# Depthwise convolution of two channel tiles: one matmul per two taps and 64 channels, or four column groups of 32 channels with four taps in the rows

## The chip, the core and the metric

The kernel runs on one core of a Trainium2 chip. The metric is the device time of one execution in microseconds (us). The core's engines run side by side and meet at semaphores: TensorE (PE, with its weight loads shown apart as PEld), VectorE (DVE), ScalarE (ACT), GpSimd (POOL), and SyncE (SP), which here only issues DMAs.

## What is computed

A trunk of two layers over 528 positions (16 meta tokens and 512 frames) of 1024 channels, in float32. The change lies in layer 0's mixer, whose convolution group is, cut to what matters:

```python
z = h @ w_in                                   # 1024 -> 1536
a = a_in[..., :512] * sigmoid(a_in[..., 512:]) # GLU
lhs = pad(a, 30 zeros in front)                # causal
a = conv(lhs, w[31, 512], one filter per channel) + b
a = silu(layer_norm(a, g, b))                  # over the 512 channels
...                                            # pool group p, 4 groups of 128
return concatenate([a, p]) @ w_out
```

So each of the 512 channels is filtered with its own 31 taps. After this mixer come a feed-forward block, a gated linear attention layer, a second feed-forward block and a last norm; they are not touched.

## The kernel before, in words

Channels lie on the 128 partitions, positions in the free dimension; the 512 convolution channels are four tiles `c` = 0 to 3 (`CT`), each 128 channels by 528 positions (`TOK`). Nearly all products are "exact" ones: both operands are split into a high and a low part (`w_hi`, `w_lo`, `u_hi`, `u_lo`), and three matmuls replace one (`exact`, L1863). ACT makes the high parts (`split_hi`, L531), DVE the low ones (`split_lo`, L538), from blocks that SP loads into `raw`, two buffers deep. PSUM has four slots (`NS`); a slot is filled by PE in the order of `plan_slots`, and PE begins slot n only when n-4 has been evacuated. Each engine's order is written out by hand, as one instruction stream.

PE's order in the mixer: for each `c` two projections (`glu`), with the transposes of the small vectors (L1991, L1992) after the first, and a transpose of the input (`flip_x`); then `conv_taps(2)`; the four pool projections `p`; `conv_taps(3)`, into whose middle `mix(0)` and `mix(1)` are put (`MIX_BEFORE`); `mix(2)`, `mix(3)`; then eight `outp` products, with `mean` after the third and `var` after the fifth; then eight `outc` products.

Where the taps run. Tiles 0 and 1 are done on DVE, one instruction for each tap over the tile (`run_taps`, L1356, the instruction at L1372 and for tap 0 at L1363), 62 in all. Of tile 2 DVE does 14 taps and PE 17, and PE does all 31 of tile 3. On PE a tile is taken as two groups `g` of 64 channels. `x_phase` holds the even positions of a group in one half of the partitions and the odd ones in the other half (`split_phases`, four ACT copies a tile, L838); `diag` holds, for each step, a 128 by 128 matrix of four diagonals with the taps (`build_diags`, two ACT instructions a step, L809, with `ident_half` and `cw_phase`); one matmul of 264 columns (L2009) is a step, 18 of them for tile 2 and 32 for tile 3, float32 without a split. ACT adds the bias and sorts even and odd positions back (`evac_conv`, four instructions a tile, L873).

`mean` needs the sum of all four tiles: DVE writes `conv_sum` in two additions (L1421, L1432), and PE waits for them and for tile 2's last tap (L2043 to L2045).

Of the kernel before, what the change touches and what calls it, by code (L numbers as in the profile page):

```python
# [20 lines left out]
P = 128  # L21
# [34 lines left out]
PHASE = P // 2  # L56
SHIFTS = {2: 9, 3: 16}
PE_TAPS = [(c, t) for c in SHIFTS for t in range(2 * SHIFTS[c] - 1)]
PE_STEPS = [(c, g, j) for c in SHIFTS for g in range(2) for j in range(SHIFTS[c])]
DIAGS = 28  # L60

MIX_BEFORE = 16
# [5 lines left out]
CONV_STEP, POOL_STEP, MIX_STEP, OUT_STEP = 11, (0, 3, 3, 0), (0, 0, 1, 0), 2  # L68
# [138 lines left out]
def build_trunk(nc, x, meta_tokens, mix_norm_g, ffn_norm_g, ffn_w1, ffn_w2, cp_w_in, cp_conv_w,  # L207
                cp_conv_b, cp_ln_g, cp_ln_b, cp_pool_w, cp_pool_scale, cp_w_out, gla_w_in,
                gla_gate_w2, gla_gate_b, gla_head_g, gla_w_out, final_norm_g, out):
    with ExitStack() as ctx:  # L210
# [47 lines left out]
        with ExitStack() as part:  # L258
# [13 lines left out]
            with ExitStack() as mixer0:  # L272
                win = sb("win", [P, 2, WMAX + TOK], F32, mixer0)
                rcount = sb("rcount", [P, WMAX], F32, mixer0)
                pw = sb("pw", [P, PG, P], F32, mixer0)
                pw_hi = sb("pw_hi", [P, PG, P], F32R, mixer0)
                pw_lo = sb("pw_lo", [P, PG, P], F32R, mixer0)


                conv_in = sb("conv_in", [P, CT, TAPS - 1 + TOK], F32, mixer0)  # L280
                conv = sb("conv", [P, CT, TOK], F32, mixer0)
                x_phase = sb("x_phase", [P, 2, 2, (TAPS - 1 + TOK) // 2], F32, mixer0)
                cw_phase = sb("cw_phase", [P, 2, 2, (TAPS + 1) // 2, 2], F32, mixer0)
                cb_phase = sb("cb_phase", [P, 2, 2], F32, mixer0)
                ident_half = sb("ident_half", [P, PHASE], F32, mixer0)
                diag = sb("diag", [P, DIAGS, 2, PHASE], F32, mixer0)
                gw2_raw = sb("gw2_raw", [P, DK], F32, mixer0)
# [40 lines left out]
        conv_sum, centred_sq_sum = h_sq[:, 0, :], h_sq[:, 1, :]  # L328
# [46 lines left out]
        x_phase_ready = sem("x_phase_ready")  # L375
        cw_phase_ready = sem("cw_phase_ready")
        phase_consts = sem("phase_consts")
        diag_ready = sem("diag_ready")
        diag_used = sem("diag_used")
# [61 lines left out]

        def diag_free(eng, i):

            c = PE_STEPS[i][0]
            if i + 1 == len(PE_STEPS) or PE_STEPS[i + 1][0] != c:
                filled(eng, SLOT["conv", c])
            else:
                eng.wait_ge(diag_used, i + 1 - (c - 2))
# [158 lines left out]
        def _(sp):  # L607
# [88 lines left out]
        def _(pool):  # L696
# [17 lines left out]
            pool.memset(ident_half[:, :], 0.0).then_inc(phase_consts, 1)  # L714
            for half in range(2):
                pool.wait_ge(phase_consts, 1 + half)
                pool.affine_select(out=ident_half[:, :], in_=ident_half[:, :], compare_op=ALU.not_equal,
                                   fill=1.0, base=-PHASE * half, pattern=[[-1, PHASE]],
                                   channel_multiplier=1).then_inc(phase_consts, 1)
            pool.memset(cw_phase[:, :, :, :, :], 0.0).then_inc(phase_consts, 1)  # L720

        @block.scalar
        def _(act):
# [65 lines left out]
            act.activation(vec[:, 2 * KD:], ps[:, n % NS, 0:NV - 2 * KD], ACT.Copy)  # L789
            act.activation(cw[:, :], ps[:, n % NS, BANK:BANK + TAPS * CT], ACT.Copy)\  # L790
# [9 lines left out]
            built = [0]  # L800

            def build_diags(count):

                for i in range(built[0], min(built[0] + count, len(PE_STEPS))):
                    c, g, j = PE_STEPS[i]
                    if i >= DIAGS:
                        diag_free(act, i - DIAGS)
                    for b in range(2):
                        last = act.activation(diag[:, i % DIAGS, b, :], ident_half[:, :], ACT.Copy,  # L809
                                              scale=cw_phase[:, c - 2, g, j, b:b + 1])  # L810
                    last.then_inc(diag_ready, 1)
                    built[0] = i + 1

            def half(i):
                return slice(PHASE * i, PHASE * (i + 1))

            def set_phases():

                taps = cw[:, :].rearrange("p (t c) -> p c t", c=CT)
                act.wait_ge(phase_consts, 4)  # L820
                for g in range(2):
                    for a in range(2):
                        act.activation(cb_phase[half(a), :, g], vec[half(g), V_CB + 2:V_CB + CT], ACT.Copy)
                        for b in range(2):
                            for c, shifts in SHIFTS.items():
                                first, last = (1 if a < b else 0), (shifts - 1 if a > b else shifts)
                                t = 2 * first + a - b
                                n = last - first
                                ins = act.activation(cw_phase[half(a), c - 2, g, first:last, b],
                                                     taps[half(g), c, t:t + 2 * n - 1:2], ACT.Copy)  # L830
                ins.then_inc(cw_phase_ready, 1)
                act.wait_ge(cw_phase_ready, 1)

            def split_phases(c):

                for g in range(2):
                    for a in range(2):
                        last = act.activation(x_phase[half(a), c - 2, g, :], conv_in[half(g), c, a::2], ACT.Copy)  # L838
                last.then_inc(x_phase_ready, 1)
# [8 lines left out]
            for c in range(CT):  # L848
# [7 lines left out]
                build_diags(6 if c else 0)  # L856
# [4 lines left out]
                if c == 0:  # L861
                    set_phases()
                if c >= 2:
                    evacuated(act, SLOT["glu", 2 * c + 1])
                    split_phases(c)

            def evac_conv(c):
# [3 lines left out]
                for g in range(2):  # L871
                    for b in range(2):
# [5 lines left out]
            build_diags(sum(c == 2 for c, _, _ in PE_STEPS) - built[0])  # L878
            evac_conv(2)
            for g in range(PG):  # L880
# [3 lines left out]
                build_diags(8 if g == 0 else 4)  # L884
                if g % 2:
                    split_hi(2 * B_POOL + g + 3)
                    split_hi(2 * B_POOL + g + 4)
                    for i in (g - 1, g):
                        act.wait_ge(pd_ready, i + 1)
                        act.activation(a_hi[:, i, :], work[i], ACT.Copy).then_inc(pd_hi_ready, 1)  # L890
                        if i == PG - 2:
                            build_diags(6)
# [7 lines left out]
            for g in range(PG):  # L900
                if g == 2:
                    build_diags(len(PE_STEPS))
                mix_hi(g)
            evac_conv(3)
# [1472 lines left out]
```

## Time and profile before

| | us |
|---|---|
| time, median of 3 runs | 1107.4 |
| time, lowest and highest | 1106.69, 1107.47 |
| span of the profiled execution | 1105.6 |
| PE busy | 1091.0 |
| PE weight loads busy | 1019.9 |
| DVE busy | 811.0 |
| ACT busy | 562.8 |
| POOL busy | 4.6 |

The span runs from the first to the last instruction of the one execution that was profiled. Busy time says how long an engine had an instruction in it; matmuls are pipelined, so a busy PE can still hide waste. The time of a stage is therefore read from the chain that ended last and from the timeline, and the work of a stage from groups of instructions.

### The profile page before, as it was taken

To read this page: it belongs to the slowest core of one execution; us is meant where nothing else is said; L and a number is where in the kernel's file an instruction comes from. 1 tells how busy PE (TensorE), PEld (TensorE's weight loads), DVE (VectorE), ACT (ScalarE), POOL (GpSimd) and SP (SyncE) were. 2 spreads that over 40 slices of the span, in tenths; PEclk is the share of its full clock that TensorE was granted. 3 is DMA by queue.
4 is the path that set the end of the run, shared out by engine and by line. 5 is a ranking of instruction groups with operands and counts; after the bars stand their busy time and mean duration, and the time that the engine had idled before them with its cause. 6 is when DMAs were issued, how large, how long until landed. Compare 5 with 4: busy or idle time off the path is not lost.

```text
span 1105.6 us, 18616 instructions
## 1 busy us (share of the span) xinstructions
PE 1091.0 (99%) x7649; PEld 1019.9 (92%) x7649; DVE 811.0 (73%) x1166; ACT 562.8 (51%) x933; POOL 4.6 (0%) x34
## 2 busy tenths in 40 slices
PE   7999999999999999999999999999999999999997
PEld 6999999999999999999999788787898898899897
DVE  6889987786786785789463456756796786786885
ACT  6658455454454454466642234534464454454564
POOL 1000000000000000000000000000000000000000
PEclk9999999999999999999999999999999999999999
DMA  7321122135134124223223211223134134234221
GB/s 213 116 76 49 58 76 88 40 115 152 39 115 129 63 83 146 77 77 114 77 78 95 75 61 39 69 84 110 43 115 147 45 115 123 68 100 130 77 76 78
DMA packets 98929, 100.39 MB, mean 91 GB/s; under 512 B 2834, under 2 KB 95692, under 8 KB 98844
## 3 DMA queue, kind: packets, MB, share of 16 engines
q1 hardware_dynamic: 98780, 99.12, 28.5%
q8 instruction: 61, 1.00, 0.4%
q14 instruction: 24, 0.20, 0.1%
q10 hardware_dynamic: 64, 0.07, 0.0%
HBM read 97.09 MB, written 2.10 MB: 90 GB/s over the span
## 4 chain that ended last, share of the span: by engine, by line
PE 97%; DVE 1%; ACT 0%; DMA 0%; issue 0%; DVEq 0%; ACTq 0%
PE ps L1876 56%; PE ps L2080 27%; PE ps L2151 4%; PE ps L2009 2%; PE ps L2232 2%; PE ps L1923 1%; PE ps L2247 1%; PE ps L2112 1%; PE ps L2181 1%; PE ps L1884 1%; DMA xin<-in_x_dram 0%; PE ps L2139 0%; DVE w_lo L577 0%; DVE sq_sum L1267 0%; PE ps L2271 0%
## 5 line engine op out<-in xcount | busy, mean ns | idle before, releaser
L1876 PE MATMUL ps<-u_lo,w_hi 128*128 128x264 f32 (+1 forms) x1120 | 298.9, 322 | 1.0 <-DVE u_lo L1328 1.0
L1876 PE MATMUL ps<-u_hi,w_hi 128*128 128x264 f32 (+1 forms) x1120 | 295.3, 320 | 0.0
L1876 PE MATMUL ps<-u_hi,w_lo 128*128 128x264 f32 (+1 forms) x1120 | 294.6, 319 | 0.0
L2080 PE MATMUL ps<-c_lo,w_hi 128*128 128x264 f32 (+1 forms) x868 | 245.9, 283 | 0.6 <-DVE w_lo L577 0.6
L2080 PE MATMUL ps<-c_hi,w_hi 128*128 128x264 f32 (+1 forms) x868 | 244.9, 282 | 0.0
L2080 PE MATMUL ps<-c_hi,w_lo 128*128 128x264 f32 (+1 forms) x868 | 244.7, 282 | 0.0
L1876 PEld LDWEIGHTS ps<-u_lo,w_hi 128*128 128x128 f32 x1120 | 184.9, 188 | 19.6 <-issue 4.2
L531 ACT ACTIVATE w_hi<-raw 128x1024 fp32r<-128x1024 f32 x118 | 123.7, 1056 | 151.8 <-PE ps L1876 134.1
L1876 PEld LDWEIGHTS ps<-u_hi,w_hi 128*128 128x128 f32 x1120 | 185.8, 188 | 16.0 <-issue 0.7
L1876 PEld LDWEIGHTS ps<-u_hi,w_lo 128*128 128x128 f32 x1120 | 185.6, 188 | 15.4
L538 DVE TENSOR_TENSOR w_lo<-raw,w_hi 128x1024 fp32r<-128x1024 f32 x118 | 143.6, 1222 | 76.5 <-ACT w_hi L531 74.4
L2080 PEld LDWEIGHTS ps<-c_lo,w_hi 128*128 128x128 f32 x868 | 163.4, 188 | 1.1 <-issue 0.8
L2080 PEld LDWEIGHTS ps<-c_hi,w_hi 128*128 128x128 f32 x868 | 163.5, 188 | 0.2
L2080 PEld LDWEIGHTS ps<-c_hi,w_lo 128*128 128x128 f32 x868 | 163.3, 188 | 0.0
L965 ACT ACTIVATE c_hi<-parts 128x528 fp32r<-128x528 f32 (+3 forms) x132 | 73.3, 575 | 90.0 <-DVE parts L1522 51.9
L1509 DVE TENSOR_TENSOR c_lo<-parts,c_hi 128x528 fp32r<-128x528 f32 (+3 forms) x132 | 81.7, 625 | 30.1 <-ACT c_hi L965 23.8
L577 DVE TENSOR_TENSOR w_lo<-s_sum,w_hi 128x1024 fp32r<-128x1024 f32 x62 | 75.7, 1221 | 11.6 <-ACT w_hi L569 11.2
L1490 DVE SCALAR_TENSOR_TENSOR relu<-ps,rstd 128x528 f32<-128x528 f32 (+1 forms) x64 | 44.7, 698 | 51.6 <-PE ps L1876 51.4
L569 ACT ACTIVATE w_hi<-s_sum 128x1024 fp32r<-128x1024 f32 x62 | 65.7, 1059 | 14.9 <-PE ps L1876 11.3
L569 ACT ACTIVATE w_hi<-raw 128x1024 fp32r<-128x1024 f32 (+1 forms) x62 | 52.4, 845 | 39.0 <-PE ps L2080 30.5
L577 DVE TENSOR_TENSOR w_lo<-raw,w_hi 128x1024 fp32r<-128x1024 f32 (+1 forms) x62 | 59.0, 952 | 9.2 <-ACT w_hi L569 9.0
L1372 DVE SCALAR_TENSOR_TENSOR conv<-conv_in,cw,conv 128x528 f32<-128x528 f32 x74 | 53.5, 763 | 0.7
(266 smaller groups left out, 1374.5 us busy)
## 6 DMA issues: line engine op xcount, KB each, us to landing
raw<-in_ffn_w_dram SPq DMA_DIRECT2D x64, 1024.0 KB, 5.4
raw<-in_gla_w_in_dram SPq DMA_DIRECT2D x12, 1024.0 KB, 5.3
raw<-in_cp_w_in_dram SPq DMA_DIRECT2D x8, 512.0 KB, 5.3
raw<-in_cp_w_out_dram SPq DMA_DIRECT2D x4, 1024.0 KB, 5.0
raw<-in_gla_w_out_dram SPq DMA_DIRECT2D x4, 1024.0 KB, 5.2
xin<-in_x_dram SPq DMA_DIRECT2D x4, 512.0 KB, 5.6
raw<-in_cp_w_in_dram SPq DMA_DIRECT2D x2, 1024.0 KB, 5.0
out_dram<-y_tok SPq DMA_DIRECT2D x4, 512.0 KB, 3.1
```

Source lines behind the costliest of these rows:

```text
L531: act.activation(w_view(w_hi, n), half_view(raw, n), ACT.Copy).then_inc(w_hi_ready, 1)
L538: dve.tensor_tensor(w_view(w_lo, n), half_view(raw, n), w_view(w_hi, n).bitcast(F32), ALU.subtract).then_inc(w_lo_ready, 1)
L569: act.activation(hi, src, ACT.Copy).then_inc(w_hi_ready, 1)
L577: dve.tensor_tensor(lo, src, hi.bitcast(F32), ALU.subtract).then_inc(w_lo_ready, 1)
L965: act.activation(c_hi[:, first:last + 1, j, 0:w], now[:, first:last + 1, :], ACT.Copy)\
L1372: V.scalar_tensor_tensor(out=conv[:, c, :], in0=src, scalar=wt, in1=conv[:, c, :], op0=ALU.mult, op1=ALU.add).then_inc(tap_done[c], 1)
L1490: V.scalar_tensor_tensor(out=relu[:, i % 2, a:b], in0=slot_ap(n, tokens), scalar=0.0, in1=rstd[:, a:b], op0=ALU.max, op1=ALU.mult)\
L1509: V.tensor_tensor(c_lo[:, first:last + 1, j, 0:w], now[:, first:last + 1, :], c_hi[:, first:last + 1, j, 0:w].bitcast(F32), ALU.subtract)\
L1876: last = mm(ps[:, n % NS, c:c + b - a], l, r[:, a - origin:b - origin], start=(k == 0 and i == 0), stop=(k == count - 1 and i == 2))
L2009: mm(ps[:, n % NS, BANK * g:BANK * g + TOK // 2], diag[:, i % DIAGS, :, :].rearrange("p b n -> p (b n)"), x_phase[:, c - 2, g, j:j + TOK / ...
L2080: last = mm(bank, l[:, 0, j, :], r, start=(fresh and j == 0 and m == 0), stop=(j == KD // 2 - 1 and m == 2), skip_group_check=not fresh)
L2151: last = mm(ps[:, n % NS, 0:256], l, r, start=(k == 0 and i == 0), stop=(k == KD - 1 and i == 2))
```

## The change

Tiles 2 and 3 are now done on PE alone, all 31 taps. A tile is taken as four groups `g` of 32 channels, and four taps are stacked in the 128 rows: `shifted[32j + p, g, t]` is channel `32g + p` at position `t + j`. It is filled by 16 DMAs from SBUF to SBUF for each tile, issued by ACT (`shift_rows`), the second tile's once the first tile's matmuls are done. A matmul has 128 rows, 32 weight columns and 264 positions, and its output lies in the PSUM partitions of its group; there are 8 rounds of four taps, two halves and four groups, 64 matmuls for a tile, the four groups innermost. The weights of a tile, `diag[:, i]`, are now made by one DVE instruction from `ident_quad` and `cw_quad`. `cw_quad` comes from a second arrangement of the taps, `quad_rows`, loaded by 16 more small DMAs on SP ahead of the second to fourth `glu` weights, turned by one more transpose on PE and copied by ACT. `evac_conv` is one ACT instruction. `mix(0)` and `mix(1)` stand ahead of `conv_taps(3)`. DVE does tiles 0 and 1 alone; `late_sum` (tiles 2 and 3) and `conv_sum` (0 and 1) are both taken by the `mean` products. POOL sets `ident_quad` in place of `ident_half`.

```diff
+QUAD = 4
+QP = P // QUAD
+ROUNDS = (TAPS + QUAD - 1) // QUAD
+PE_TILES = (2, 3)
+SHIFTED = QUAD * (ROUNDS - 1) + TOK
...
+            sp.wait_ge(quad_consts, 1)
+            for i, c in enumerate(PE_TILES):
+                for r in range(ROUNDS):
+                    at = QUAD * (ROUNDS * i + r)
+                    n = min(QUAD, TAPS - QUAD * r)
+                    sp.dma_start(quad_rows[at:at + QUAD, 0:QP * n].rearrange("g (s p) -> g s p", p=QP),
+                                 cp_conv_w[0][QUAD * r:QUAD * r + n, P * c:P * (c + 1)]
+                                 .rearrange("s (g p) -> g s p", p=QP)).then_inc(quad_loaded, 16)
             for c in range(1, CT):
                 load_glu(c)
...
+            act.activation(cw_quad[:, :, :], ps[:, n % NS, BANK + P:BANK + P + 2 * QUAD * ROUNDS]
+                           .rearrange("p (c i) -> p c i", c=len(PE_TILES)), ACT.Copy).then_inc(quad_turned, 1)
...
+            def shift_rows(c):
+
+                act.wait_ge(quad_consts, 2)
+                evacuated(act, SLOT["glu", 2 * c + 1])
+                if c != PE_TILES[0]:
+                    filled(act, SLOT["conv", c - 1])
+                for j in range(QUAD):
+                    for g in range(QUAD):
+                        act.dma_start(shifted[QP * j:QP * (j + 1), g, :],
+                                      conv_in[QP * g:QP * (g + 1), c, j:j + SHIFTED]).then_inc(shifted_loaded, 16)
...
-                for g in range(2):
-                    for b in range(2):
-                        last = act.activation(conv[half(g), c, b::2],
-                                              ps[half(b), n % NS, BANK * g:BANK * g + TOK // 2], ACT.Identity,
-                                              bias=cb_phase[half(b), c - 2, g:g + 1])
-                last.then_inc(evac[n % NS], 1)
...
+                act.activation(conv[:, c, :], slot_ap(n), ACT.Identity, bias=vec[:, V_CB + c:V_CB + c + 1])\
+                   .then_inc(evac[n % NS], 1)
+
             evac_conv(2)
+            shift_rows(3)
...
+            def build_diags(i):
+
+                dve.wait_ge(quad_consts, QUAD + 3)
+                dve.wait_ge(quad_turned, 1)
+                size = [P, QUAD * ROUNDS, QP]
+                V.tensor_tensor(diag[:, i, :, :], ident_quad[:, None, :].to_broadcast(size),
+                                cw_quad[:, i, :, None].to_broadcast(size), ALU.mult).then_inc(diag_ready, 1)
...
+                    pe.wait_ge(quad_loaded, 16 * len(PE_TILES) * ROUNDS)
+                    flip(ps[:, n % NS, BANK + P:BANK + P + 2 * QUAD * ROUNDS], quad_rows[:, :], 2 * QUAD * ROUNDS)
...
-                pe.wait_ge(x_phase_ready, c - 1)
-                mine = [i for i, step in enumerate(PE_STEPS) if step[0] == c]
-                for i in mine:
-                    if i == len(PE_STEPS) - MIX_BEFORE:
-                        mix(0)
-                        mix(1)
-                    _, g, j = PE_STEPS[i]
-                    pe.wait_ge(diag_ready, i + 1)
-                    mm(ps[:, n % NS, BANK * g:BANK * g + TOK // 2],
-                       diag[:, i % DIAGS, :, :].rearrange("p b n -> p (b n)"),
-                       x_phase[:, c - 2, g, j:j + TOK // 2], start=(j == 0), stop=(j == SHIFTS[c] - 1))\
-                        .then_inc(filled_n if i == mine[-1] else diag_used, 1)
+                i = PE_TILES.index(c)
+                pe.wait_ge(diag_ready, i + 1)
+                pe.wait_ge(shifted_loaded, 16 * QUAD * QUAD * (i + 1))
+                for r in range(ROUNDS):
+                    for at, a, b in parts(FULL):
+                        for g in range(QUAD):
+                            last = mm(ps[QP * g:QP * (g + 1), n % NS, at:at + b - a], diag[:, i, QUAD * r + g, :],
+                                      shifted[:, g, QUAD * r + a:QUAD * r + b], start=(r == 0), stop=(r == ROUNDS - 1))
+                last.then_inc(filled_n, 1)
...
+            mix(0)
+            mix(1)
             conv_taps(3)
...
-                    evacuated(pe, SLOT["conv", 2])
-                    pe.wait_ge(tap_done[2], sum((2, t) not in PE_TAPS for t in range(TAPS)))
-                    plain(n, [(ones_c[:, :], conv_sum), (ones_c[:, :], conv[:, 2, :])], FULL)
+                    plain(n, [(ones_c[:, :], late_sum), (ones_c[:, :], conv_sum)], FULL)
```

## Rows read from the trace of the kernel before

**Rows 1.** The page: busy time of each engine; granted TensorE clock in 40 slices.

```profile
PE 1091.0 (99%) x7649; PEld 1019.9 (92%) x7649; DVE 811.0 (73%) x1166; ACT 562.8 (51%) x933; POOL 4.6 (0%) x34
...
PEclk9999999999999999999999999999999999999999
```

**Rows 2.** Chain that ended last, in order: start, us, what (67 to 145 us).

```profile
67.69 8.02 PE ps L2009 x36
75.70 23.35 PE ps L1876 x192
99.05 7.12 PE ps L2009 x32
106.18 1.45 PE ps L1876 x12
107.63 7.12 PE ps L2009 x32
114.75 10.35 PE ps L1876 x84
125.10 1.78 PE ps L1884 x8
126.88 5.85 PE ps L1876 x48
```

**Rows 3.** All instructions of line 2009: count, duration in ns, first and last start.

```profile
L2009 PEld LDWEIGHTS ps<-x_phase,diag x100: 187/189/192, 67.4 to 114.1; 128*128 128x128 f32 x100
L2009 PE MATMUL ps<-x_phase,diag x100: 383/385/388, 67.5 to 114.4; 128*128 128x264 f32 x100
```

**Rows 4.** Timeline of PE and its weight loads where line 2009 begins: start, us.

```profile
67.42 0.52 PEld L2009 LDWEIGHTS ps<-x_phase,diag 128*128 128x128 f32 x3
67.52 0.61 PE L2009 MATMUL ps<-x_phase,diag 128*128 128x264 f32 x2
```

**Rows 5.** Timeline of PE: eight shortest float32 matmuls in a row, and the next.

```profile
525.00 0.95 PE L1918 MATMUL ps<-ones_d,sq_sum 128*128 128x1 f32 x8
525.80 0.47 PE L1884 MATMUL ps<-sq_sum,ones_d 128*128 128x264 f32 x1
```

**Rows 6.** Weight loads of 64 columns, and of 128: duration in ns.

```profile
L2181 PEld LDWEIGHTS ps<-w_lo,um_both x32: 133/134/136, 535.7 to 577.5; 128*64 128x64 f32 x32
L1918 PEld LDWEIGHTS ps<-ones_d,sq_sum x8: 188/192/192, 524.9 to 525.7; 128*128 128x128 f32 x8
```

**Rows 7.** Timeline of SP's DMA issues ahead of the second glu weights.

```profile
10.16 0.29 SPq L659 DMA_DIRECT2D vec_rows<-in_cp_pool_scale_dram  x1
10.50 0.30 SPq L659 DMA_DIRECT2D vec_rows<-in_gla_gate_b_dram  x1
...
12.42 2.22 SPq L669 DMA_DIRECT2D gw_raw<-in_gla_gate_w_dram  x4
14.69 0.42 SPq L634 DMA_DIRECT2D raw<-in_cp_w_in_dram  x1
```

**Rows 8.** DMA issues: KB each, us from issue to landing.

```profile
raw<-in_cp_w_in_dram SPq DMA_DIRECT2D x8, 512.0 KB, 5.3
gw_raw<-in_gla_gate_w_dram SPq DMA_DIRECT2D x4, 32.0 KB, 2.4
xmeta<-in_meta_tokens_dram ACTq DMA_DIRECT2D x1, 64.0 KB, 3.5
```

**Rows 9.** Timeline of PE: the transposes of the small vectors.

```profile
22.78 0.26 PE L1923 MATMUL ps<-ident,vec_rows 46*128 46x46 f32 x1
22.97 0.32 PE L1923 MATMUL ps<-ident,cw_rows 124*128 124x124 f32 x1
```

**Rows 10.** Timeline of ACT: its own DMA issues; then around the copies of tile 2.

```profile
1.18 0.44 ACTq L753 DMA_DIRECT2D gain_rows<-in_mix_norm_g_dram  x1
...
56.23 1.85 ACT L838 ACTIVATE x_phase<-conv_in 64x279 f32<-64x279 f32 x4
61.01 0.61 ACT L854 ACTIVATE act<-ps 128x528 f32<-128x528 f32 x1 [2.93 <-PE ps L1876]
```

**Rows 11.** Timeline of DVE, from the second pool group to the third mix.

```profile
88.05 0.71 DVE L1395 TENSOR_TENSOR win<-pin 128x528 f32<-128x528 f32 x1 [1.46 <-ACT pin L883]
...
108.01 1.32 DVE L1413 TENSOR_TENSOR a_lo<-act,a_hi 128x528 fp32r<-128x528 f32 x2
```

**Rows 12.** Groups by line: busy us, mean ns, then idle before them.

```profile
L1372 DVE SCALAR_TENSOR_TENSOR conv<-conv_in,cw,conv 128x528 f32<-128x528 f32 x74 | 53.5, 763 | 0.7
L809 ACT ACTIVATE diag<-ident_half,cw_phase 128x64 f32<-128x64 f32 x100 | 24.8, 335 | 0.0
```

More of the change, by code:

```diff
@@ L53 @@
 C0 = BANK - SPLIT
[L56 to L62, printed above, removed]
+QUAD = 4
[3 more added lines that the diff above has]
+SHIFTED = QUAD * (ROUNDS - 1) + TOK
 OUT_MEAN, OUT_VAR = 3, 5
 SHARE = 256
-CONV_STEP, POOL_STEP, MIX_STEP, OUT_STEP = 11, (0, 3, 3, 0), (0, 0, 1, 0), 2
+CONV_STEP, POOL_STEP, MIX_STEP = 11, (0, 3, 3, 0), 4
 V_MIX, V_FFN, V_FIN = 0, 2 * KD, 4 * KD
@@ L326, in build_trunk @@
         work = [relu[:, 0, :], relu[:, 1, :], act2[:, 0, :], act2[:, 1, :]]
-        conv_sum, centred_sq_sum = h_sq[:, 0, :], h_sq[:, 1, :]
+        conv_sum, late_sum, centred_sq_sum = h_sq[:, 0, :], h_sq[:, 1, :], h_sq[:, 1, :]
         x_normed = h[:, :, :].rearrange("p k t -> p (k t)")[:, 0:TT * D].rearrange(
@@ L713, in _ @@
             last.then_inc(consts, 3)
[L714 to L720, printed above, removed]
+            pool.memset(quad_rows[:, :], 0.0).then_inc(quad_consts, 1)
+            pool.memset(conv_in[:, :, TAPS - 1 + TOK:], 0.0).then_inc(quad_consts, 1)
+            pool.memset(ident_quad[:, :], 0.0).then_inc(quad_consts, 1)
+            for i in range(QUAD):
+                pool.wait_ge(quad_consts, 3 + i)
+                pool.affine_select(out=ident_quad[:, :], in_=ident_quad[:, :], compare_op=ALU.not_equal,
+                                   fill=1.0, base=-QP * i, pattern=[[-1, QP]],
+                                   channel_multiplier=1).then_inc(quad_consts, 1)
         @block.scalar
@@ L814, in half @@
[L814 to L820, printed above, removed]
-                for g in range(2):
[L822 to L839, printed above, removed]
+            def shift_rows(c):
[7 more added lines that the diff above has]
+                                      conv_in[QP * g:QP * (g + 1), c, j:j + SHIFTED]).then_inc(shifted_loaded, 16)
@@ L1346, in _ @@
                             gw2[at:at + RANK, :].bitcast(F32), ALU.subtract).then_inc(small_lo, 1)
-            taps = {c: [t for t in range(TAPS) if (c, t) not in PE_TAPS] for c in range(CT)}
+            taps = {c: list(range(TAPS)) for c in range(CT) if c not in PE_TILES}
             last_tile = [0]
@@ L1359, in run_taps @@
                     src, wt = conv_in[:, c, t:t + TOK], cw[:, t * CT + c:t * CT + c + 1]
-                    done = sum((c, i) not in PE_TAPS for i in range(t))
                     if t == 0:
@@ L1365, in run_taps @@
                         continue
[L1366 to L1371 removed]
+                    dve.wait_ge(tap_done[c], t)
                     V.scalar_tensor_tensor(out=conv[:, c, :], in0=src, scalar=wt, in1=conv[:, c, :],
                                            op0=ALU.mult, op1=ALU.add).then_inc(tap_done[c], 1)
+            def build_diags(i):
[4 more added lines that the diff above has]
+                                cw_quad[:, i, :, None].to_broadcast(size), ALU.mult).then_inc(diag_ready, 1)
             for c in range(CT):
@@ L1417, in _ @@
                 if g == 2:
-                    run_taps(2 * TAPS, (0, 1))
-                    dve.wait_ge(tap_done[0], TAPS)
-                    dve.wait_ge(tap_done[1], TAPS)
-                    V.tensor_tensor(conv_sum, conv[:, 0, :], conv[:, 1, :], ALU.add).then_inc(conv_summed, 1)
-                run_taps(MIX_STEP[g], (0, 1, 2))
+                    run_taps(MIX_STEP, (0, 1))
                 dve.wait_ge(mix_hi_ready, g + 1)
@@ L1427, in _ @@
                                        op1=ALU.subtract).then_inc(evac[n % NS], 1)
-            run_taps(2 * TAPS, (0, 1, 2))
-            dve.wait_ge(conv_summed, 1)
-            evacuated(dve, SLOT["conv", 3])
-            V.tensor_tensor(conv_sum, conv_sum, conv[:, 3, :], ALU.add).then_inc(conv_summed, 1)
+            for c in PE_TILES:
+                evacuated(dve, SLOT["conv", c])
+            V.tensor_tensor(late_sum, conv[:, 2, :], conv[:, 3, :], ALU.add).then_inc(conv_summed, 1)
+            run_taps(2 * TAPS, (0, 1))
+            dve.wait_ge(tap_done[0], TAPS)
+            dve.wait_ge(tap_done[1], TAPS)
+            V.tensor_tensor(conv_sum, conv[:, 0, :], conv[:, 1, :], ALU.add).then_inc(conv_summed, 1)
             def out_pool(k):
```

68 lines of the change are left out of this document (18 added, 50 removed).

## The prediction, made before the changed kernel was run

> **What bounds the kernel now.** I read the page first: PE is busy for 99% of the span, DVE for 73%, ACT for 51%, and the granted clock stays at its upper level of 2.4 GHz [rows 1]. So a microsecond taken from PE's stream is worth a microsecond, unless PE then waits for something else. The chain that ended last tells where the touched work lies: from 67.7 to beyond 130 us it is PE alone, with no gap, so neither ACT nor DVE holds PE there now [rows 2]. In that stretch the convolution's matmuls take three pieces, 8.02 + 7.12 + 7.12 = 22.3 us. DVE's taps (74 at 763 ns) and ACT's diagonals (100 at 335 ns) lie beside it [rows 12]. The question is thus what the new matmuls cost PE; what DVE and ACT are spared is worth nothing by itself.
>
> **PE's convolution work.** Line 2009 has 50 steps but 100 matmul and 100 load records: each float32 matmul shows as two pairs of load and matmul [rows 3]. 22.3 us / 100 = 0.223 us for each pair of 264 columns, 0.445 for a matmul. The loads are hidden: by 67.8 us three loads have started and two matmuls, so a load runs while the matmul before it streams [rows 4].
>
> After the change there are 8 rounds x 2 halves x 4 groups = 64 matmuls a tile, 128 in all, again of 264 columns: 256 pairs where there were 100. Only side by side work in different column groups can pay for that. No row of before shows two matmuls side by side, so this is bounded from both sides:
> - Nothing overlaps: 256 x 0.223 = 57.0 us, that is 34.7 more.
> - All four groups overlap fully: 57.0 / 4 = 14.3 us, 8.0 less.
> - The middle: PE takes its stream in order. Each matmul is two passes, a then b, in the same group, and they stand behind each other. Pass b of group 0 must wait until pass a of group 0 has streamed, 0.223 us. Group 1's pass a stands behind it. If a matmul never starts ahead of one issued before it, only b of one group and a of the next run together. Each matmul then costs one pass: 128 x 0.223 = 28.5 us, 6.2 more.
>
> I take the middle. The order of the records (load, matmul, load, matmul on one bank) is what rows 3 and 4 show, and nowhere in the trace does a later matmul record begin before an earlier one. It lies between ends that are 43 us apart, and both stay as rivals.
>
> The Trainium skill bears on this in "TensorE: Matmul & The Clock Gate", Part 3, What overlaps and what doesn't. It says that matmuls of different tiles run at the same time but begin and end in program order. By that rule the sum is the middle one. Its measured 2.38x for three column groups has one pass for each group, so it doesn't show this case. The same section says that a weight load overlaps a running matmul only when its row group differs. All loads here use all rows, and rows 4 speaks against it, since loads there are hidden on the same rows; by that sentence loads would come on top and the time would lie above my forecast.
>
> Changing between 128 and 32 weight columns I cost at nothing; the 64 column loads in this kernel are shorter than those of 128 (134 against 192 ns) and none shows idle time [rows 6]. A few tenths either way are in the range.
>
> **The start.** SP issues 16 small DMAs between the last `gw_raw` and the second tile's `glu` weights, which were issued at 14.69. The `vec_rows` loads of 2 KB come every 0.34 us, those of `gw_raw` every 0.6 (2.22 / 4 = 0.56 busy) [rows 7]. At 0.34 the last is issued at 14.69 + 15 x 0.34 = 19.8 and lands, with `gw_raw`'s 2.4 us, at 22.2 [rows 8]. PE reaches the transposes at 22.78 [rows 9], so nothing is lost. At 0.6 it lands at 26.1 and PE waits 3.3 us. The size and row count are those of `vec_rows`, so I stay near the lower end and take 0.4. The added transpose is some 0.1 (the distance between the two there is 0.19). Behind them the weights are issued at 20.1 instead of 14.69 and land 5.3 later, at 25.4 [rows 8]; high and low part add 1.1 and 1.2, so they are ready at 27.7, and PE wants them about 30.0. That is hidden with 2.3 to spare. At 0.6 they are ready at 31.9, but PE is then 3.3 late itself. Start: +0.5, bounds 0.1 and 3.4.
>
> **The shifted rows.** For tile 2 ACT issues 16 DMAs from where the `x_phase` copies stood, 56.2. Its own issues take 0.44 each [rows 10]; the last goes out at 62.8. There is no SBUF to SBUF transfer in the trace. With the 3.5 us of `xmeta`'s 64 KB [rows 8], near to these 71 KB, it lands at 66.3; PE wants it at 67.5, after half a microsecond of start delay even later. Cost 0. With 0.6 an issue and 5.3 to land it would be 70.5, 3 us late: the upper bound. ACT's sigmoid of the last glu pair slips from 61.0 to 63.3 [rows 10], and DVE's product with it by about 2; behind it stand only taps and pool work that is not due for 10 us. Tile 3's 16 issues start when tile 2's matmuls are done, and its rows are wanted 25 us later. They hold ACT for 7.0 us, just as PE does the first pool projection (5.8), so the first `pin` copy is up to 1 us late; hidden.
>
> **Off the path.** DVE drops 14 taps (10.7 us) and gets two products of 128 x 1024, 2.4 us. ACT drops the diagonals (24.8 us) and the phase copies. The 62 taps of tiles 0 and 1 are used up before the mixes, as 50 + 12 calls. `late_sum` and `conv_sum` take 1.4 us after `mix(3)`, and PE has three `outp` products (8.8 us) until `mean`. No gain there, since PE did not wait before [rows 2].
>
> **Sum.** +6.2 (matmuls) + 0.5 (start) + 0 (shift) = +6.7. On the profiled span of 1105.6 that is 1112.3. The median of the runs is 1.8 above that span, so 1114.1; I say 1114.
>
> **Rival A, full overlap in four groups (faster).** If PE holds work of each group apart, a group's pass b does not stop the next group's pass a: -8.0. It needs a pair every 0.056 us. The densest in the trace is 0.10: eight one-column matmuls in 0.80 [rows 5]. But those carry loads of 128 columns and loads of fewer are shorter [rows 6], so it neither excludes 0.056 nor shows it; at 0.10 the conv would take 25.6 us, slower than before. Then DVE holds PE: from 88.05 it runs on to 109.3, when the low parts for `mix(2)` and `mix(3)` are written [rows 11]. PE would come to `mix(2)` at 67.7 + 7.1 + 23.4 + 1.5 + 7.1 + 0.5 = 107.3, and the first of the two is ready near 107.9, DVE starting its chain some 0.8 earlier. That gives back about 0.7: -8.0 + 0.7 + 0.5 = -6.8, 1100.6.
>
> **Rival B, no overlap (much slower).** One matmul after the other, as in every row of before: +34.7 + 0.5 = +35.2, 1142.6. Against it: that is then no use of column groups at all, and the change does not do what it says.
>
> **Rival C, between A and the forecast.** Overlap limited by how fast pairs can be taken, some 0.08 us: 20.5 us, -1.8 + 0.5, with the shift or start wait near zero in sum: about 1107.
>
> **Point of decision.** The pair period in the new stage: 22.3 / 256 = 0.087 us is break-even for the matmuls alone, and 0.085 with the 0.5 at the start; below that the change wins, above it loses.
>
> **How the numbers follow.** Forecast 0.45, A 0.34, B 0.14, C 0.07. What can be told from no change is 0.2%, 2.2 us. Faster: A and some of C, 0.36. Same: the rest of C, 0.05. Slower: forecast and B, 0.59. The range must reach A, with 2 us below for a smaller wait at the mix: 1099. Above the forecast it takes the two upper bounds of start and shift (3 + 3) and partly exposed loads: 1124. Left out is B, and a little beyond the ends. The forecast's own range is 1111 to 1124.
>
> **What would show it.** In the profile of after: PE's stage from 67.5 to the first pool projection takes 14.3 us (7.1 for A, 28.5 for B); matmul starts come in twos, 0.22 apart; the convolution has 256 matmul records. The vector transposes start near 23.2. A wait of PE for DMA `shifted` would show step three wrong, a wait for DVE's `a_lo` at `mix(2)` would speak for A.

## The result, and the profile after

| | before | after |
|---|---|---|
| time, median, us | 1107.3 (13 runs) | 1109.1 (13 runs) |
| lowest, highest, us | 1106.57, 1107.47 | 1107.75, 1112.27 |
| span of the profiled execution, us | 1105.6 | 1107.7 |

The ratio of the times is 1.002, 95% interval 1.0012 to 1.0028: the changed kernel is 1.8 us slower, and its runs spread over 4.5 us where those of before spread over 0.9. Its three longest runs (1110.59 to 1112.27) have a mean granted clock of 0.993; the runs of before have 0.998 or 0.999. In the profile PE has less to do than before and the kernel is not faster:

```profile
PE 1084.4 (98%) x7806; PEld 1010.6 (91%) x7806; DVE 803.3 (73%) x1154; ACT 530.4 (48%) x800; POOL 4.9 (0%) x37
```

Against [rows 1] PE is busy 6.6 us less, and its share fell from 99% to 98%. So the matmuls paid, and something gave it back as waits. The convolution's matmuls, the line that answers to [rows 3], and the timeline of PE cut at 71.6 us, which answers to [rows 4]:

```profile
L1969 PEld LDWEIGHTS ps<-shifted,diag x256: 106/110/110, 71.3 to 110.3; 128*32 128x32 f32 x128
L1969 PE MATMUL ps<-shifted,diag x256: 382/386/410, 71.3 to 110.5; 128*32 128x264 f32 x128
```

```profile
71.31 0.65 PE L1969 MATMUL ps<-shifted,diag 128*32 128x264 f32 x8 [0.90 <-DMA shifted<-conv_in]
```

There are 256 records of 264 columns, each with the duration that they had before (386 ns against 385). A record is one pass of a matmul, and each float32 matmul has two. But eight of them have begun within 0.3 us of the first, where [rows 4] has two. The raw records give the pattern: four start within 20 ns (71.312, 71.319, 71.326 and 71.332 us), and the next four begin at 71.534, 0.22 us later. So the passes of four groups stream together. The chain that ended last (start, us, what) has the first tile, and then the stretch that answers to the end of [rows 2]:

```profile
71.31 7.36 PE ps L1969 x128
...
116.49 11.11 PE ps L1836 x78
127.59 1.78 PE ps L1844 x8
129.38 5.84 PE ps L1836 x48
```

A tile takes 7.36 us, the second one 7.33 by the timeline: 14.7 us where [rows 2] has 22.3. That is 7.6 us less. Yet the `mean` products start at 127.59, against 125.10 in [rows 2]. What PE waited for in the first 150 us (who waits, for whom: us in total, times, longest), the small waits left out:

```profile
PE ps L1836 <- DVE a_lo L1376: 4.4, 1, 4.4
PE ps L1836 <- ACT act L825: 2.8, 1, 2.8
...
PE ps L1969 <- DMA shifted<-conv_in: 0.9, 1, 0.9
```

**The wait of 2.8 us, at the start.** Timelines of SP, ACT and PE:

```profile
14.40 5.47 SPq L665 DMA_DIRECT2D quad_rows<-in_cp_conv_w_dram  x16
19.91 3.65 SPq L624 DMA_DIRECT2D raw<-in_cp_w_in_dram  x4
```

```profile
27.19 1.06 ACT L521 ACTIVATE w_hi<-raw 128x1024 fp32r<-128x1024 f32 x1 [3.63 <-DMA raw<-in_cp_w_in_dram]
...
31.75 0.61 ACT L825 ACTIVATE act<-ps 128x528 f32<-128x528 f32 x1
```

```profile
32.51 0.48 PE L1836 MATMUL ps<-u_lo,w_hi 128*128 128x264 f32 x2 [2.75 <-ACT act L825]
```

The second tile's `glu` weights are issued at 19.91 instead of 14.69 [rows 7] and ACT can round them from 27.19 on. The sigmoid that empties the first tile's `glu` slot stands behind that in ACT's stream. PE, at its fifth slot, needs the first of the four emptied, and waits for the sigmoid.

**The wait of 4.4 us, at the third mix.** Timeline of ACT, which answers to [rows 10], and of PE:

```profile
59.37 10.36 ACTq L809 DMA_DIRECT2D shifted<-conv_in  x16
69.82 0.61 ACT L825 ACTIVATE act<-ps 128x528 f32<-128x528 f32 x1 [10.77 <-PE ps L1836]
...
78.78 10.22 ACTq L809 DMA_DIRECT2D shifted<-conv_in  x16
89.05 0.61 ACT L846 ACTIVATE pin<-ps 128x528 f32<-128x528 f32 x1 [9.65 <-issue]
```

```profile
115.28 0.48 PE L1836 MATMUL ps<-a_lo,pw_hi 128*128 128x264 f32 x2 [4.37 <-DVE a_lo L1376]
```

Sixteen issues take ACT over 10 us, 0.64 each. They push the last sigmoid to 69.8 and the first `pin` copy to 89.05. Both hold DVE: its last 17 taps ahead of the pool work come behind the last `glu` product, which needs that sigmoid, and the first pool sum needs the first `pin`. DVE's pool work ends with the low parts (`a_lo`) that the third mix reads.

**The clock behind that wait.** Windows of PE's granted clock (window, length, busy us of the engines, then the clock):

```profile
111.20:115.20 4.00, 0.00 (x0) 0.00 (x0) 3.93 (x8) 2.42 (x4) 0.00 (x0) 1.00 0.00 0
115.20:116.50 1.30, 1.00 (x7) 0.79 (x7) 1.30 (x3) 0.18 (x1) 0.00 (x0) 0.84 0.37 60
116.50:118.00 1.50, 1.50 (x7) 1.50 (x8) 1.32 (x2) 0.52 (x1) 0.00 (x0) 0.50 1.05 407
118.00:120.00 2.00, 2.00 (x12) 2.00 (x12) 1.04 (x2) 0.70 (x1) 0.00 (x0) 0.62 0.47 180
```

The clock is still at the upper level while PE waits and when it resumes. It then falls to 0.50, the lower level of 1.2 GHz. The windows with 0.84 and 0.62 are mixtures: the clock record has the lower level from 116.1 to 119.5 us. From the third mix to `mean` PE needs 127.59 - 115.28 = 12.3 us for what took 10.35 [rows 2].

| where | us against before |
|---|---|
| first `glu` matmul (16.43 against 16.77) | -0.3 |
| waits for the glu slot | +2.8 |
| wait for `shifted` | +0.9 |
| two tiles' matmuls | -7.6 |
| wait at the third mix | +4.4 |
| third mix to `mean`, in part at the lower clock | +2.0 |
| the rest, not traced piece by piece (the added transpose is in it) | +0.3 |
| `mean` begins later by | +2.5 |

Of those 2.5 us 2.1 are left at the end of the span.

### The profile page after: what moved, and what is told of

It is laid out like the page before. It is cut to its first block, busy times and chain, and to the rows that moved or that the text cites. A ratio compares the mean times of both kernels' runs of the same rounds, so it can differ in the third digit from the quotient of the medians.

```text
span 1107.7 us, 18839 instructions
## 1 busy us (share of the span) xinstructions
PE 1084.4 (98%) x7806; PEld 1010.6 (91%) x7806; DVE 803.3 (73%) x1154; ACT 530.4 (48%) x800; POOL 4.9 (0%) x37
## 3 DMA queue, kind: packets, MB, share of 16 engines
q1 hardware_dynamic: 99092, 99.15, 28.5%
## 4 chain that ended last, share of the span: by engine, by line
PE 90%; DVE 3%; ACTq 2%; SPq 2%; issue 1%; ACT 1%; DMA 1%; DVEq 0%
PE ps L1836 51%; PE ps L2039 27%; PE ps L2110 4%; ACTq L809 2%; PE ps L2191 2%; PE ps L2206 1%; PE ps L2071 1%; DVE conv L1325 1%; PE ps L2140 1%; PE ps L1969 1%; DMA raw<-in_cp_w_in_dram 1%; PE ps L1844 1%; DVE win L1358 1%; PE ps L1883 1%; SPq L665 0%
## 5 line engine op out<-in xcount | busy, mean ns | idle before, releaser
L1325 DVE SCALAR_TENSOR_TENSOR conv<-conv_in,cw,conv 128x528 f32<-128x528 f32 x60 | 43.1, 763 | 0.5
## 6 DMA issues: line engine op xcount, KB each, us to landing
shifted<-conv_in ACTq DMA_DIRECT2D x32, 69.5 KB, 3.1
```

Source lines behind the costliest of these rows:

```text
L1325: V.scalar_tensor_tensor(out=conv[:, c, :], in0=src, scalar=wt, in1=conv[:, c, :], op0=ALU.mult, op1=ALU.add).then_inc(tap_done[c], 1)
```

## The experiments

The theory that the profile suggests: the matmuls gain what the full overlap promises, and three separate side effects of the DMAs (late weights at the start, late rows for tile 2, tile 3's issues on ACT) give it back. The rival: the waits are only where PE would now wait anyway, because DVE can't be ready sooner.

**e1_glu_first: the second tile's weights ahead of the 16 small DMAs.**

```diff
+            load_glu(1)
             sp.wait_ge(quad_consts, 1)
...
-            for c in range(1, CT):
+            for c in range(2, CT):
```

> SP issues the second tile's glu weights ahead of the 16 small tap DMAs; nothing else changes. Theory (queues): the 2.75 us in which PE waited for the sigmoid's evacuation at 29.8 came from ACT, which stood in order behind the late weights. Then that wait goes, PE loses at most 1 us at the vector transposes for the small DMAs that now land later, and the time falls by 1.5 to 3 us against the changed kernel, to about 1106.5. Rival: the late sigmoid is covered by later slack (the mix wait of 4.4 us is set by DVE, which also starts earlier or not): no change, 1109.

1106.71 us, ratio to before 0.9997 (0.9988 to 1.0007): 2.4 below the changed kernel, as the theory has it. The wait for the sigmoid is gone from PE's waits; the one at the mix stands:

```profile
PE ps L1837 <- DVE a_lo L1377: 4.3, 1, 4.3
```

**e2_tile3_sp: tile 3's sixteen issues on SP.**

```diff
+            shift_from(sp, 3, (0, 1, 2, 3))
...
             evac_conv(2)
-            shift_rows(3)
```

> Tile 3's 16 shift DMAs are issued by SP in place of ACT; nothing else changes. Theory (queues): ACT's 10.3 us of issuing held back the first pool copy from about 84.9 to 89.05, with it DVE's pool chain, and PE's 4.4 us at the third mix and the lower clock behind it. Then the first pool copy stands near 84.9, the mix wait is under 1 us, the granted clock stays at its upper level, and the time falls by 5 to 6.5 us, to about 1103. Rival (DVE work): DVE's own chain from the first pool copy to the mixes is too long for a shorter PE stage whoever issues the DMAs; the wait stays above 3 us and the gain is under 2 us.

1108.53 us, ratio 1.0016 (1.0007 to 1.0025): only 0.6 gained, which is not clear of the noise, since the changed kernel's interval is 1.0012 to 1.0028. The theory's 5 to 6.5 us were wrong; the outcome is the rival's (a wait above 3 us, a gain under 2). ACT copies `pin` at 82.91 now, 6.1 us sooner, but PE still waits 4.0 us at the third mix. ACT's timeline, then DVE's:

```profile
68.05 0.61 ACT L826 ACTIVATE act<-ps 128x528 f32<-128x528 f32 x1 [10.67 <-PE ps L1836]
...
82.91 0.61 ACT L846 ACTIVATE pin<-ps 128x528 f32<-128x528 f32 x1 [5.32 <-PE ps L1836]
```

```profile
74.89 1.22 DVE L539 TENSOR_TENSOR w_lo<-raw,w_hi 128x1024 fp32r<-128x1024 f32 x1
76.02 11.64 DVE L1325 SCALAR_TENSOR_TENSOR conv<-conv_in,cw,conv 128x528 f32<-128x528 f32 x17
87.57 0.71 DVE L1358 TENSOR_TENSOR win<-pin 128x528 f32<-128x528 f32 x1
```

DVE doesn't wait for `pin` any more. It comes to it at 87.57 only, since 17 taps stand ahead of it in its stream, and those begin late because the last sigmoid is still late (68.05). Two delays lay side by side; taking one away shows the other. That DVE is 2.2 us earlier at the pool work than in the changed kernel (89.76) is largely chance: in this execution ACT could start on the second tile's weights 5.6 us after their issue, in the other 7.3, with the same issues ahead of them, and the sigmoids came 1.7 us earlier. PE came to the third mix earlier too.

**e3_tile2_split: half of tile 2's issues on SP.**

```diff
+            shift_from(sp, 2, (2, 3))
...
-                    shift_rows(c)
+                    shift_from(act, c, (0, 1))
```

> Of tile 2's 16 shift DMAs SP issues eight (ahead of its next weight load) and ACT eight. Theory (queues): an issue takes 0.64 us on its engine, so the rows are there 5 us earlier and PE's wait of 1.1 us at the tile's first matmul goes: 0.8 to 1.1 us less, about 1108. Rival (the transfers themselves are what takes the time, since all run on the same DMA engines): no gain.

1108.38 us, ratio 1.0014 (1.0005 to 1.0024). The wait for `shifted` is gone. The 0.7 us gained are near the 0.8 that was expected, but like e2_tile3_sp's they are not clear of the noise. The wait at the third mix is 4.4 us as in the changed kernel, with tile 3's issues still on ACT.

**e4_all: the three together.**

> All three together. Theory (queues): the three waits were all that stood against the shorter matmuls; the sum is 8 to 10 us less than the changed kernel, 1099 to 1101, which is 6 to 8 us under the kernel before. Rival (DVE work): at most 4 us less, about 1105.

1102.53 us, ratio 0.9963 (0.9950 to 0.9976). That is above the rival's 4 us and short of the 8 to 10 expected. One by one the three gave 2.4 + 0.6 + 0.7 = 3.7 us; together they give 6.6. The difference is the wait at the third mix, which needs both the early sigmoid and the early `pin`, and which is down to 1.4. With it the fall of the clock behind it is gone: each of the three edits alone shows one in its profile, and here the clock is 1.00 from 107 to 116 us. What PE still waited for:

```profile
PE ps L1838 <- DVE a_lo L1378: 1.4, 1, 1.4
PE ps L1838 <- DVE a_lo L1385: 0.2, 1, 0.2
```

**e5_lean and e9_tile3_sp_lean: fewer taps ahead of the pool chain.** One edit, on e4_all and on e2_tile3_sp:

```diff
-CONV_STEP, POOL_STEP, MIX_STEP = 11, (0, 3, 3, 0), 4
+CONV_STEP, POOL_STEP, MIX_STEP = 5, (0, 3, 3, 0), 0
```

> e4_all, and 6 of DVE's taps of tiles 0 and 1 (CONV_STEP 11 to 5) moved from ahead of the pool chain to behind the mixes. Theory (DVE reaches the pool chain too late): in e4_all PE still waits 1.4 + 0.2 us for a_lo at the mixes; 6 taps are 4.6 us, so the wait goes and the time falls by 1.3 to 2 us, to about 1101. Rival (the pool copies, which follow PE itself, set the start of DVE's chain): no change, 1102.5.

> The changed kernel with tile 3's shift DMAs on SP (as in e2_tile3_sp) and 6 taps moved behind the mixes. In e2_tile3_sp the first pool copy came at 82.9 but DVE reached it at 87.6 only, since its last glu product had waited for a sigmoid that ACT gave at 68.05, behind tile 2's issues. Theory (two things held DVE's chain at the same time, ACT's issues for tile 3 and the taps that the late sigmoid pushed back): with both eased the chain starts 4 us earlier, the mix wait falls from 4.0 to under 0.5 us, the clock stays up, and the time falls by 4.5 to 6 us, to about 1103. Rival: DVE's chain from there on is the bound; under 2 us.

On e4_all it does next to nothing: 1101.96 us, ratio 0.9951 (0.9937 to 0.9964), and 1.2 us of the wait remain, against the expectation that it would vanish. On e2_tile3_sp it gives 4.4 us, just short of the 4.5 expected: 1104.09, ratio 0.9975 (0.9965 to 0.9984). So the taps ahead of `pin` were what held DVE in e2_tile3_sp, and the wait at the third mix falls from 4.0 to 1.2 there (under 0.5 was expected). This run also gives a price for the clock. Timeline of PE at its third mix, then the chain at `mean`:

```profile
111.95 0.48 PE L1836 MATMUL ps<-a_lo,pw_hi 128*128 128x264 f32 x2 [1.22 <-DVE a_lo L1376]
```

```profile
122.91 1.78 PE ps L1844 x8
```

From the third mix to `mean` it takes 122.91 - 111.95 = 11.0 us, against 12.3 in the changed kernel, and its windows over that stretch show the upper level throughout. Both have the same wait of 0.2 us at the fourth mix. So 1.4 of the 2.0 us in the table above are the clock's. In e1_glu_first, e2_tile3_sp and e3_tile2_split, whose clock fell too, the stretch took 11.9, 12.5 and 11.8 us, so the price differs from run to run.

**e6_groups_outer, e6b_groups_then_halves: how far PE looks ahead.** Both are e4_all with the loops of the convolution in another order:

```diff
-                for r in range(ROUNDS):
-                    for at, a, b in parts(FULL):
-                        for g in range(QUAD):
+                for g in range(QUAD):
+                    for r in range(ROUNDS):
+                        for at, a, b in parts(FULL):
```

```diff
-                    for at, a, b in parts(FULL):
-                        for g in range(QUAD):
+                    for g in range(QUAD):
+                        for at, a, b in parts(FULL):
```

> e4_all with the four column groups outermost: a group's 16 matmuls (32 pairs of load and matmul) stand together before the next group's. Theory (each group has a stream of its own, which PE fills from its queue ahead of order as far as the queue reaches): the next group's instructions are 64 further on, so little overlaps; a tile takes 25 to 28.5 us in place of 7.3, the time is 1138 to 1145. Rival (PE looks ahead without a bound that matters here): 7.3 us a tile, no change, 1102.5.

> e4_all with the groups outside the two halves, inside the rounds: two matmuls (four pairs) of one group in a row. Theory (queue per group, lookahead of some tens of instructions): overlap as before, 7.3 to 8 us a tile, about 1102.5. Rival (one stream in order, in which only the four first starts looked free): a group's four passes hold the next group's back; 5 x 0.223 - ... three of four passes alone, some 20 to 24 us a tile, 1130 or more.

Groups outermost: 1137.65 us. Four passes of a group behind each other (two halves of two passes), then the next group: 1101.94. Both are single runs. The chain of the first, both tiles, and of the second, its first tile:

```profile
68.11 26.02 PE ps L1971 x128
...
119.14 26.02 PE ps L1971 x128
```

```profile
67.92 7.33 PE ps L1971 x128
```

With 32 passes of a group in a row almost all overlap is lost: 26.02 us of the 128 x 0.223 = 28.5 that one after the other would take. The 2.5 us that it is shorter, over three changes of group, are 0.8 us or some four passes a change. The raw records show the same: the starts come singly, 0.22 us apart, except at the three changes, where the last four passes of a group each have one of the next group's within 0.03 us. Four in a row of one group cost nothing, and there the second, third and fourth group start beside the first although 4, 8 and 12 passes stand ahead of them. This is the case that strict order excludes whatever the order of the two passes inside a matmul: in order, three passes of each group's four would run alone, 20 us or more a tile. Both runs fit a hold of about four passes for each group; what holds them is not shown.

**e7_two_groups: the two upper groups left out.** `for g in range(2)` on e4_all. It leaves out the matmuls of channels 64 to 127 of each of the two tiles.

> e4_all without the matmuls of column groups 2 and 3: half of the tile's channels are not convolved (that part of the computation is left out), 64 matmuls in all in place of 128. Theory (a group's own streaming sets the stage: 32 passes of 0.223 us each): a tile still takes 7.2 us, and the time stays within 0.5 us of e4_all. Rival (the rate at which PE takes pairs, 0.057 us, sets it): a tile takes 3.6 us; PE then only waits longer for DVE, and the stage itself shows it.

```profile
67.90 7.24 PE ps L1971 x64
```

Half the matmuls take the same 7.24 us (64 records for this tile, 128 for both), and the time of this single run is 1101.98. So neither loads nor issue set the time of a tile, but the 32 passes that one group has to stream: 32 x 0.223 = 7.1.

**e8_quads_early: the second `glu` weights and the small tap DMAs ahead of `pw`, `rw` and `gw_raw`**, on e5_lean, whose profile shows 1.1 us of waiting for the taps' transpose:

```diff
-            sp.dma_start(pw[:, :, :], cp_pool_w[0].rearrange("g c d -> c g d")).then_inc(small_loaded, 16)
...
             load_glu(1)
...
+            sp.dma_start(pw[:, :, :], cp_pool_w[0].rearrange("g c d -> c g d")).then_inc(small_loaded, 16)
```

> e5_lean with the second tile's glu weights and the 16 small tap DMAs issued ahead of the pool, rank and gate weights. Theory: PE's 0.5 us at the vector transposes goes, and no other wait comes, since those weights are wanted after 24 us: 0.3 to 0.5 us less than e5_lean. Rival (the moved loads collide with the x tiles or the first glu weights, or small_loaded comes late and holds ACT's sigmoid): slower by up to 1 us.

1101.80 us, ratio 0.9948 (0.9935 to 0.9962). The transposes' wait is gone, and the time is the same as e5_lean's within 0.2 us; the 0.3 to 0.5 expected are not seen. PE comes earlier to the third mix and waits 1.2 us there again. This is the lowest median of the study, 5.5 us below the kernel before and 7.3 below the changed one.

**e10_lo_first: DVE's two `a_lo` ahead of its two `split_lo`**, on e8_quads_early:

```diff
-                    split_lo(2 * B_POOL + g + 3)
-                    split_lo(2 * B_POOL + g + 4)
                     for i in (g - 1, g):
...
+                    split_lo(2 * B_POOL + g + 3)
+                    split_lo(2 * B_POOL + g + 4)
```

> The quads-early kernel with one more move: VectorE computes the two low parts of the pooled tile pair (1.32 us for both) ahead of the two split_lo steps of the pointwise weights (2.36 us), not behind them. If the remaining 1.2 us that PE waits at the third mix slot is VectorE's order alone, that wait goes to 0.1 or less and the time falls by 1.0 to 1.5 us, to about 1100.6. Rival: the pooled high parts come from ACT late (101.66 and 105.53 in the run before), VectorE now stands idle for the second of them, and the weights' low parts behind it are late for the same slot: then the wait is as long as before under another name, and the time stays at 1101.8.

1102.15 us, ratio 0.9952 (0.9937 to 0.9966): no gain. The wait at the third mix is gone, and PE waits 1.87 us one slot later instead, for the `a_lo` that DVE writes from the first mix's slot, behind the two `split_lo` that were moved. The rival was right in the outcome, not in its way: DVE doesn't stand idle for ACT. PE's timeline, and its clock after the wait, from an execution that was the longest of the five (1103.47):

```profile
107.24 0.51 PE L1838 MATMUL ps<-a_lo,pw_hi 128*128 128x264 f32 x2
...
110.12 0.51 PE L1838 MATMUL ps<-a_lo,pw_hi 128*128 128x264 f32 x2 [1.87 <-DVE a_lo L1385]
```

```profile
110.10:114.00 3.90, 3.88 (x19) 3.88 (x20) 3.03 (x5) 0.70 (x1) 0.00 (x0) 0.56 0.81 269
```

**e11_pool_lean: four taps fewer inside the pool chain**, on e8_quads_early, with `POOL_STEP` from `(0, 3, 3, 0)` to `(0, 1, 1, 0)`.

> The quads-early kernel with VectorE's fill-in taps ahead of pool groups 1 and 2 cut from three each to one each; the four taps go behind the mixes. If the 1.2 us that PE still waits at the third mix slot are VectorE's place for its taps, four taps of 0.69 us (2.8 us) less ahead of it make the wait 0 to 0.2. But VectorE is busy for 21.7 of the 22 us from 88 to 110, and the same taps must be done before the mean products: its sum is then ready near 118.4 as before, PE comes there at 117.9 and waits about 0.5. Time 0.6 to 1.0 us lower, near 1101.0. Rival: VectorE's total sets the end, the whole wait moves from the mix to the mean products (1.2 us there), and the time stays at 1101.8.

1104.16 us, ratio 0.9971 (0.9961 to 0.9982): 2.4 slower than e8_quads_early. The profiled execution was the shortest of the eight (1102.60), so it explains less than 1 of these 2.4 us; the rest lies in executions that were not profiled. The first half of the expectation holds: the third mix waits for nothing. The second half doesn't. The wait turns up ahead of `mean`, and it is longer. PE's timeline, and DVE's:

```profile
119.84 2.02 PE L1846 MATMUL ps<-h_sq,ones_c 128*128 128x264 f32 x8 [2.26 <-DVE h_sq L1396]
```

```profile
87.13 0.71 DVE L1360 TENSOR_TENSOR win<-pin 128x528 f32<-128x528 f32 x1 [2.82 <-ACT pin L848]
```

With fewer taps DVE stands idle for 2.8 us until the second `pin` comes (1.5 in e8_quads_early), and has to do the taps later. They are work that `mean` needs, so in this order moving them moves the wait. In e8_quads_early DVE is busy almost without a gap on the way from `pin` to the mixes:

```profile
88.00:110.00 22.00, 20.53 (x235) 16.93 (x235) 21.72 (x36) 9.38 (x14) 0.00 (x0) 1.00 0.16 57
```

That is 21.72 of 22 us (third busy time). This doesn't show that the last 1.2 us of waiting belong to DVE's load and not to its order. Ahead of that stretch DVE stands idle for 4.9 us, since six taps had been moved away from there (0.9 us in e4_all). And in e4_all it has room behind the mixes. The timeline of DVE in e8_quads_early, and in e4_all the sum over tiles 0 and 1 and what follows:

```profile
81.82 0.71 DVE L1360 TENSOR_TENSOR win<-pin 128x528 f32<-128x528 f32 x1 [4.89 <-ACT pin L848]
```

```profile
113.52 0.70 DVE L1396 TENSOR_TENSOR h_sq<-conv 128x528 f32<-128x528 f32 x1
...
117.33 0.70 DVE L1256 TENSOR_TENSOR h<-h,ps 128x528 f32<-128x528 f32 x1 [2.21 <-PE ps L1838]
```

`mean` comes at 120.2 there, 6 us after that sum, and it comes at 120.2 in e5_lean too, which has six taps behind the mixes. So e4_all with `POOL_STEP` as in e11_pool_lean and `MIX_STEP` 0 could do the four taps (2.8 us) behind the mixes without making `mean` late. That order was not run, and whether it takes the last wait away is open.

## Why the prediction was wrong

The forecast was 1114.0 us, slower by 6.7. The range of 1099 to 1124 holds the measured 1109.1. The time lies between its cases, and for a reason that none of them has: the matmuls went as in rival A and the waits far beyond it. Rival C's 1107 is nearest by luck, since its price of a pass, 0.08 us, isn't what was measured (14.7 / 256 = 0.057).

**PE's convolution work: the step that failed.** The price of a pass was right (0.223 us) and so was the count, 256. The failure is the sentence that a pass b of group 0 holds up the pass a of group 1. It was taken from [rows 3] and [rows 4], and from no matmul in the trace starting ahead of an earlier one. But the records stand in the order of their starts and don't say which was issued first. And the matmuls of before that use fewer than 128 weight columns in a row, the 96 records at L2139 and L2181, all write the same 64 partitions, so the rows could not show the case. The trace of after shows four passes starting within 20 ns, though the two passes of a matmul belong to the same group. e6b_groups_then_halves shows it with four passes of a group in a row, still at 7.33 us a tile: a pass of another group starts ahead of passes issued before it. The two tiles take 14.7 us against 28.5 forecast and 14.3 in rival A. e7_two_groups shows that this is the floor of one group's own stream. The Trainium skill says in "TensorE: Matmul & The Clock Gate", Part 3, What overlaps and what doesn't, that matmuls of different tiles begin and end in program order. e6b_groups_then_halves differs from it as to the beginning, and the measurement decides; e6_groups_outer shows what is left of order, since with 32 passes of a group ahead the next group starts late.

**The start: right terms, wrong waiter.** SP's sixteen issues took 5.47 us (5.4 forecast), the transposes didn't wait for the taps, and the weights were issued at 19.91 (20.1). ACT could use them 1.8 us later than forecast (27.2 instead of 25.4). The argument then asked when PE wants the second tile's weights, and found 2.3 us of cover. It did not ask what stands behind those weights in ACT's stream: the sigmoid that frees the slot PE needs first. The cost was 2.8 us instead of 0.5, inside the bound of 3.4. e1_glu_first gives 2.4 of it back.

**The shifted rows: the issue was mis-sized.** 0.44 us each was ACT's only issue of before [rows 10]; the new ones took 0.64. Landing in 3.1 us was near the 3.5 taken. Tile 2 cost 0.9 us instead of 0.

**Tile 3's issues: dismissed in a sentence.** "up to 1 us late; hidden" was worked out for PE's projection alone, with the 7.0 us of the low issue price. ACT was held for 10.2 us, `pin` came at 89.05, and the work that follows it is DVE's chain to the third mix, the very chain that rival A names as the next bound. Rival A let it begin 0.8 us early; it began late instead, and the wait was 4.4 us where 0.7 was put down. e2_tile3_sp and e3_tile2_split each left that wait in place, e4_all took most of it: the last sigmoid, pushed by tile 2's issues, and `pin`, pushed by tile 3's, both held it.

**The clock: in no case of the sum.** A stall of PE was priced at its own length. Here the stage behind it ran 1.4 us longer for the lower level.

**Right.** No wait at `mean` with `late_sum` and `conv_sum`; the marks named for A (a stage of about 7.3 us a tile, a wait for `a_lo` at the third mix) are what the profile shows. The direction is as forecast, by an accident of two errors of opposite sign: 14 us too much for the matmuls, some 10 too little for the waits and the clock.

## What to carry to other kernels

When PE's work shrinks, walk the streams of the engines that feed it again, each instruction in order: a DMA issue or a wait for late weights delays whatever stands behind it, most of all an evacuation that frees a PSUM slot. Price delays that end at the same consumer together, for taking away one of two may show next to nothing (0.6 and 0.7 us alone, with the start's 2.4 they made 6.6). And when work is moved out of a full stretch, look for where it goes: two reorderings here only moved PE's wait (1.2 us at the third mix became 1.9 one slot later, or 2.3 at `mean`), while DVE stood idle for 4.9 us ahead of that stretch.

## What the runs showed of the hardware

- Four float32 matmul streams, each to its own 32 columns of PE, run fully side by side if they are mixed finely: a tile of 128 passes takes 7.3 us, as long as the 32 passes of one group, and 7.24 with half of the groups left out. Four passes of one group in a row cost nothing, 32 in a row cost 18.7 us a tile (26.02 against 7.33).
- Weight loads of 32 columns take 110 ns each by the records and stay hidden, at 128 of them in 7.3 us (0.057 us apiece). Since 128 x 0.110 is 14 us, they must overlap each other too.
- A transfer from SBUF to SBUF of 32 partitions (69.5 KB) took 0.64 us to issue on ACT and the same on SP (10.32 us for 16), against 0.34 for a 2 KB load from memory; it landed 3.1 us after its issue.
- The granted clock fell to 0.50 at the end of PE's waits or within 1.3 us behind them for waits of 4.4 us in the changed kernel, 4.3 in e1_glu_first, 4.0 in e2_tile3_sp, 4.4 and 3.1 in e3_tile2_split and 1.9 in e10_lo_first (a mean of 0.56 over the next 3.9 us). It stayed at 1.00 behind the 2.8 us at the start of the changed kernel, the 2.6 at the start of e9_tile3_sp_lean, the 2.3 of e11_pool_lean and every wait of 1.2 to 1.4. So the length of the one wait doesn't decide it: 1.9 us cost the upper level (PE was busy for 1.24 of the 3.1 us before it went on) and 2.8 did not.
- Loads of 512 KB issued behind sixteen small ones were usable 7.3 us after their issue in one execution and 5.6 in another (the changed kernel and e2_tile3_sp, with the same issues ahead).
